# Two column tiles and four sums for the second-half correction of a delta-rule recurrence, and semaphores cleared inside the next block

## Chip, cores and metric

The kernel runs on one core of a Trainium2 chip. The metric is the device time of one execution in microseconds, lower is better. TensorE is PE in the profile (PEld its weight loads), VectorE is DVE, ScalarE is ACT, GpSimd is POOL, and SP is the engine that issues most transfers. A `q` behind an engine's name means its sequencer: waits, branches, drains.

## What is computed

One kernel computes a whole stack for 512 tokens of width 1024: a mixer with a two-directional RWKV-7 recurrence and multi-scale pooling, a product-key expert layer (8 heads, 16 of 16384 experts), a differential-attention layer and a gated-linear-attention layer, each of the two with memory cross-attention and a convolutional feed-forward. The part that the first half of the change touches is the recurrence, cut from the reference:

```python
def wkv7_scan(r, w, k, v, kk, a, reverse):
    def step(state, inp):
        r_t, w_t, k_t, v_t, kk_t, a_t = inp
        sa = jnp.einsum('bhvk,bhk->bhv', state, -kk_t)
        state = (state * w_t[:, :, None, :]
                 + sa[..., :, None] * (kk_t * a_t)[..., None, :]
                 + v_t[..., :, None] * k_t[..., None, :])
        out = jnp.einsum('bhvk,bhk->bhv', state, r_t)
        return state, out
    ...
    _, out = lax.scan(step, state0, xs, reverse=reverse)

for d in range(N_DIR):            # forward, then backward
    ...
    o = o + wkv7_scan(rh, heads(decay), kd, vh, kk, heads(a), reverse=(d == 1))
```

There are 8 heads of 64 channels, two directions, and 512 steps.

## The kernel before

The program is a row of blocks (`nc.Block()`), in each of which every engine runs its own instruction stream and waits on semaphores of the others. A block ends in a barrier of all engines.

**The recurrence** is `mixer_scan`. It works in chunks of 128 steps, four of them (`ST = 4`), and on two heads (`h`) at a time: `m` runs over the four pairs of heads and `d` over the two directions, so there are eight turns, one behind the other. A turn is `solve` and then `steps`. `solve` inverts, for all four chunks and both heads, the triangular matrix of each chunk. It does so by halves of 64 steps: `inverse_t` holds the inverses of the two diagonal 64x64 blocks, made in five levels of products (`E` and `T`, lines L1938 and L1949). Then it applies the inverse to `rhs[d]`, which holds two blocks of 64 columns for each of the two heads, for 128 rows (steps) of each chunk:

- `C{h}` (L1955, copied back by DVE at L1809): the block below the diagonal times the inverse of its half.
- `Y{h}` (L1959): both halves of the right-hand sides times their own inverses. ACT copies the result into `rhs[d]` (L1756).
- `X{h}` (L1965): the correction of the second half, which is the product of `C` with the solved first half, for each chunk. It needs C{h} and Y{h}. DVE adds it to `rhs[d]` (L1813).

`first_half` and `second_half` are rows 0 to 63 and 64 to 127 in the forward direction, and the other way round in the backward one. `ps` are the eight PSUM banks. `steps` then transposes the first columns of `rhs[d]` (`z_t`, L1972), copies the others for the first chunk (`sa0`, L1822), and goes through the four chunks in order, with a state that is handed from one to the next. Between its steps PE, DVE and ACT do pieces of the next turn's front (`beside`): transposes (L1867), and the matrices Lt, L, zk, qb, qk (L1894 to L1900).

Between engines the order is kept by `Steps`: an engine ends each named step with an increment of its semaphore, and the waits count the steps by name. PE's instruction order is the order of the code. An fp32 matmul stands in the trace as two records.

**Semaphores.** Each block takes new ones with `c.semaphore`, which collects them in `c.taken`. When many are in use, `clear_semaphores` (L118 to L122) has POOL clear those in `c.taken` and frees their numbers, behind the barrier that ends a block, and then all engines meet in a second barrier (L121) before the next block begins. `c.apart` holds those that a stream made ahead of time keeps across this. It is called in four places: behind the recurrence, behind the first part of the experts, and behind the attention of each of the two last layers. The blocks that follow are `norm_and_out` (mixer's output, names `gn_`, `out0`), the experts' second part (`ev_`), `residual_split` (`out_`, attention's output product) and `memory_and_out`. Nothing is cleared between the first feed-forward and `project_gla` (names `glav_`).

## Time and profile before

| | us |
|---|---|
| median of 3 runs | 3103.48 |
| lowest and highest | 3098.47, 3103.51 |
| the profiled execution, its own time | 3100.74 |
| its span in the trace | 3099.0 |
| mean granted TensorE clock in it | 0.991 |

The recurrence's eight turns, some 28 us each, lie from 170 to 398 us. The four barriers that `clear_semaphores` adds lie at 398, 1313, 2069 and 2658 us. All times of the trace are from the start of the span. In a timeline row the columns are the start, the time taken together by the rows that it merges, the engine, the line, the operation, what it writes and reads, the count, and in brackets how long the engine sat idle before it and what ended that.

### The profile page before, as it was taken

How to read it: one execution, taken by the hardware profiler on the slowest of the kernel's cores; microseconds unless marked ns; L12 is line 12 of the kernel's file. 1: busy time of each engine (PE TensorE's matmuls, PEld its weight loads, DVE VectorE, ACT ScalarE, POOL GpSimd, SP SyncE). 2: the span in 40 equal slices, each digit the busy share in tenths (PEclk: the TensorE clock that was granted, in tenths of full speed). 3: DMA queues.
4: the chain of work that ended last, by engine and by line, in shares of the span. 5: the costliest groups of instructions: out<-in, count | busy, mean ns of one | idle time of the engine just before them, and what ended most of it. 6: DMA issues, size and time to landing. Idle time of an engine off the chain costs nothing. (4 is left out here: it accounts for less than half of the span.)

```text
span 3099.0 us, 55557 instructions
## 1 busy us (share of the span) xinstructions
PE 3003.1 (97%) x20135; PEld 2648.1 (85%) x20135; DVE 2218.0 (72%) x3931; ACT 965.5 (31%) x1789; POOL 1137.1 (37%) x808
## 2 busy tenths in 40 slices
PE   8999989899999999999999999999999999899999
PEld 6678868799999999999999997768888878588887
DVE  7766687788898898688888886577775345577741
ACT  2444421333434334333333333461211023321110
POOL 5244335222222122144333334214555443245553
PEclk9999999999999999999999999999999999899999
DMA  4100023377878877899999963112223241122333
GB/s 163 34 3 3 3 82 107 118 236 255 297 248 264 287 248 268 289 378 359 349 354 339 352 216 100 38 48 94 96 95 95 79 99 35 55 89 95 99 91 94
DMA packets 241745, 507.91 MB, mean 164 GB/s; under 512 B 44534, under 2 KB 135814, under 8 KB 238124
## 3 DMA queue, kind: packets, MB, share of 16 engines
q1 hardware_dynamic: 182828, 321.11, 31.2%
q0 software_dynamic: 36864, 134.23, 13.3%
q10 hardware_dynamic: 21888, 50.34, 4.2%
q8 instruction: 106, 1.74, 0.2%
q14 instruction: 59, 0.48, 0.0%
HBM read 453.17 MB, written 52.44 MB: 163 GB/s over the span
## 5 line engine op out<-in xcount | busy, mean ns | idle before, releaser
L198 POOL TENSOR_TENSOR up_low<-normed,up_high 128x1024 fp32r<-128x1024 f32 (+1 forms) x136 | 317.2, 2332 | 300.6 <-DVE up_high L193 300.6
L3039 POOL DMA_INDIRECT ev_rows<-in_v,ev_list x128 | 180.1, 1407 | 321.1 <-DVE ev_row_sum L3106 307.7
L203 PE MATMUL up_ps<-ffn_high,up_high 128*128 128x512 f32 x704 | 274.9, 390 | 3.0 <-DVEq L828 3.0
L205 PE MATMUL up_ps<-ffn_high,up_low 128*128 128x512 f32 x704 | 273.9, 389 | 0.0
L204 PE MATMUL up_ps<-ffn_low,up_high 128*128 128x512 f32 x704 | 273.9, 389 | 0.0
L203 PE MATMUL eu_ps<-norm_unit_high,expert_high 128*128 128x384 f32 x768 | 265.4, 346 | 0.0
L205 PE MATMUL eu_ps<-norm_unit_high,expert_low 128*128 128x384 f32 x768 | 257.9, 336 | 0.0
L204 PE MATMUL eu_ps<-norm_unit_low,expert_high 128*128 128x384 f32 x768 | 257.7, 336 | 0.0
L193 DVE CAST up_high<-normed 128x1024 fp32r<-128x1024 f32 (+1 forms) x136 | 91.7, 675 | 206.2 <-PE up_down_ps L205 150.6
L2716 POOL DMA_INDIRECT expert_scores<-in_u,eu_list x64 | 84.2, 1316 | 268.5 <-DVE eu_dots L2744 260.2
L3064 ACT ACTIVATE expert_high<-mixed 128x1024 fp32r<-128x1024 f32 x95 | 100.8, 1061 | 228.9 <-PE ev_acc L205 208.7
L203 PE MATMUL ev_acc<-ev_w_high,expert_high 128*128 128x384 f32 x512 | 171.0, 334 | 0.0
L204 PE MATMUL ev_acc<-ev_w_low,expert_high 128*128 128x384 f32 x512 | 171.0, 334 | 0.0
L205 PE MATMUL ev_acc<-ev_w_high,expert_low 128*128 128x384 f32 x512 | 171.0, 334 | 0.0
L2739 DVE TENSOR_TENSOR expert_low<-eu_turned,expert_high 128x512 fp32r<-128x512 f32 x192 | 123.7, 686 | 64.6 <-ACT expert_high L2833 63.5
L3106 DVE SCALAR_TENSOR_TENSOR ev_row_sum<-ev_rows,ev_weight,ev_row_sum 128x1024 f32<-128x1024 f32 x128 | 164.3, 1285 | 3.9 <-DMA ev_rows<-in_v,ev_list 3.9
L2843 ACT ACTIVATE mixed<-eu_ps 128x384 f32<-128x384 f32 x128 | 62.9, 491 | 328.1 <-PE eu_ps L205 328.1
L2716 POOL DMA_INDIRECT normed<-in_u,eu_list x64 | 68.8, 1075 | 255.5 <-DVE eu_dots L2744 254.9
L786 ACT ACTIVATE mixed<-up_ps,columns_sb 128x512 f32<-128x512 f32 x88 | 68.6, 780 | 297.2 <-DVE up_ps L816 297.2
L3099 DVE TENSOR_TENSOR expert_low<-mixed,expert_high 128x1024 fp32r<-128x1024 f32 x95 | 118.4, 1246 | 58.6 <-ACT expert_high L3064 58.6
L203 PEld LDWEIGHTS up_ps<-ffn_high,up_high 128*128 128x128 f32 x704 | 132.2, 188 | 31.5 <-DVEq L828 3.7
L204 PEld LDWEIGHTS up_ps<-ffn_low,up_high 128*128 128x128 f32 x704 | 132.2, 188 | 27.8 <-issue 0.5
(709 smaller groups left out, 8615.5 us busy)
## 6 DMA issues: line engine op xcount, KB each, us to landing
mixed<-in_v SPq DMA_DIRECT2D x128, 512.0 KB
normed<-in_u SPq DMA_DIRECT2D x125, 512.0 KB
normed<-in_w_up SPq DMA_DIRECT2D x88, 512.0 KB, 3.4
expert_act<-mixed ACTq DMA_DIRECT2D x128, 192.0 KB
expert_gates<-eu_gates ACTq DMA_DIRECT2D x24, 1024.0 KB
expert_scores<-expert_gates SPq DMA_DIRECT2D x16, 1536.0 KB
normed<-expert_act SPq DMA_DIRECT2D x128, 192.0 KB
normed<-in_w_down SPq DMA_DIRECT2D x32, 448.0 KB, 3.3
```

The lines of the kernel that those rows point to most:

```text
L193: return nc.vector.tensor_copy(high.bitcast(F32R), of)
L198: return nc.gpsimd.tensor_tensor(low.bitcast(F32R), of, high, ALU.subtract)
L203: nc.tensor.matmul(out, w_high.bitcast(F32R), x_high.bitcast(F32R), start=start, stop=False)
L204: nc.tensor.matmul(out, w_high.bitcast(F32R), x_low.bitcast(F32R), start=False, stop=False)
L205: return nc.tensor.matmul(out, w_low.bitcast(F32R), x_high.bitcast(F32R), start=False, stop=stop)
L786: nc.scalar.activation(cv[:, s, :], ps[s][:, :], ACT.Identity, scale=c.cols[:, bass.ds(j + at + 2 * 2 * FT, 1)], bias=c.cols[:, bass.ds(j ...
L2716: nc.gpsimd.indirect_dma_start(rows[b % 4], None, u, bass.IndirectOffsetOnAxis(ap=list_[:, b % 8:b % 8 + 1], axis=0)).then_inc(fetched[b % ...
L2739: nc.vector.tensor_tensor(low[b % SLOTS][:, ks, :].bitcast(F32R), ps_u[n][:, :, :], high[b % SLOTS][:, ks, :], ALU.subtract).then_inc(low_ ...
L3039: nc.gpsimd.indirect_dma_start(rows[:, b % 4, :], None, v, bass.IndirectOffsetOnAxis(ap=list_[:, b % 8:b % 8 + 1], axis=0)).then_inc(fetch ...
L3064: nc.scalar.activation(high[b % SLOTS][:, :, :].bitcast(F32R), raw[:, b % 4, :, :], ACT.Copy).then_inc(high_made, 1)
L3099: nc.vector.tensor_tensor(low[b % SLOTS][:, :, :].bitcast(F32R), raw[:, b % 4, :, :], high[b % SLOTS][:, :, :], ALU.subtract).then_inc(low ...
L3106: nc.vector.scalar_tensor_tensor(out=row_sum[:, b % 2, :], in0=rows[:, b % 4, :], scalar=weight[:, bass.ds(i * per + b, 1)], in1=row_sum[: ...
```

## The change

In the recurrence, the correction of the second half changes on PE and DVE. Before, PE makes the four chunks of head 0 as soon as C0 and Y0 are there, all into the same 64 output rows, and then those of head 1. Afterwards PE waits for C and Y of both heads and then goes through the chunks in two groups of two (`p`). In each chunk it makes head 0 and head 1 one behind the other, each in output rows (and so columns of the array) of its own: `column_tile[d][0]` is the second half, `column_tile[d][1]` the first. There are still eight matmuls. The two groups have banks of their own (`x_bank`). DVE makes four sums (X0 to X3), each of two chunks of one head, where it made two of four chunks. Head 1's sums read PSUM rows of the other half than those that they write. The steps behind wait for X3 in place of X1.

The second part: `clear_semaphores` becomes `retire_semaphores`, which only renames the list, and `clear_stale`, which POOL runs as its first action in the next block. The second barrier is gone in all four places. There is a fifth retirement, behind the first feed-forward, whose clearing lies in `project_gla`; so that this one is possible, the semaphores of the stream and of the norm that live on are set apart in `build`.

```diff
-def clear_semaphores(nc, c):
-    nc.clear_and_free_semaphores(c.taken)
-    nc.all_engine_barrier()
-    c.taken, c.apart = c.apart, []
+def retire_semaphores(c):
+    assert not c.stale
+    c.stale, c.taken, c.apart = c.taken, c.apart, []
+
+def clear_stale(nc, c):
+    nc.clear_and_free_semaphores(c.stale)
+    c.stale = []
...
             @block.gpsimd
             def _(pool):
+                clear_stale(nc, c)
...
+        x_bank = ((ps[3], ps[1]), (ps[4], ps[5]))
+        column_tile = ((half[1], half[0]), (half[0], half[1]))
...
-                    for h in range(2):
-                        mine = rhs[d][second_half[d], :, h:4:2, :]
-                        pe_s[d].wait(dve, m, f"X{h}")
-                        done.ends(nc.vector.tensor_tensor(mine, pair(c_bank[h][second_half[d], :, :]), mine, ALU.add), f"X{h}")
+                    for p in range(2):
+                        for h in range(2):
+                            mine = rhs[d][second_half[d], 2 * p:2 * p + 2, h:4:2, :]
+                            pe_s[d].wait(dve, m, f"X{2 * p + h}")
+                            done.ends(nc.vector.tensor_tensor(mine, pair(x_bank[p][h][column_tile[d][h], 0:2, :]), mine, ALU.add), f"X{2 * p + h}")
...
                     for h in range(2):
                         dve_s[d].wait(pe, m, f"C{h}")
                         act_s[d].wait(pe, m, f"Y{h}")
-                        for t in range(ST):
-                            ins = nc.tensor.matmul(c_bank[h][two_, t, :], square[one, ST * h + t, HEAD:P], rhs[d][one, t, h:4:2, :], start=True, stop=True)
-                        pe_s[d].ends(ins, f"X{h}")
+                    for p in range(2):
+                        for t in (2 * p, 2 * p + 1):
+                            for h in range(2):
+                                ins = nc.tensor.matmul(x_bank[p][h][column_tile[d][h], t % 2, :], square[one, ST * h + t, HEAD:P], rhs[d][one, t, h:4:2, :], start=True, stop=True)
+                                if t % 2:
+                                    pe_s[d].ends(ins, f"X{2 * p + h}")
```

PE, first turn, from the last products Y to the transposes for z_t. `L1965` is X before, `L1978` after; `L1867` the next turn's first transposes; `L1972` and `L1986` z_t. Before:

```order
628 L1959 MATMUL scan_ps<-scan_rhs,scan_inverse_t 64x128 x8
629 L1965 MATMUL scan_ps<-scan_rhs,normed 64x128 [waits scan_scalar_done0,scan_vector_done0]
630 L1965 MATMUL scan_ps<-scan_rhs,normed 64x128 x3
631 L1965 MATMUL scan_ps<-scan_rhs,normed 64x128 [waits scan_scalar_done0,scan_vector_done0]
632 L1965 MATMUL scan_ps<-scan_rhs,normed 64x128 x3
633 L1867 MATMUL scan_ps<-ident,scan_ez 128x128 [waits scan_vector_done1]
634 L1867 MATMUL scan_ps<-ident,scan_ez 128x128 x3
635 L1972 MATMUL scan_ps<-ident,scan_rhs 128x128 [waits scan_vector_done0]
```

After:

```order
628 L1970 MATMUL scan_ps<-scan_rhs,scan_inverse_t 64x128 x8
629 L1978 MATMUL scan_ps<-scan_rhs,normed 64x128 [waits scan_vector_done0,scan_scalar_done0]
630 L1978 MATMUL scan_ps<-scan_rhs,normed 64x128 x7
631 L1878 MATMUL scan_ps<-ident,scan_ez 128x128 [waits scan_vector_done1]
632 L1878 MATMUL scan_ps<-ident,scan_ez 128x128 x3
633 L1986 MATMUL scan_ps<-ident,scan_rhs 128x128 [waits scan_vector_done0]
```

All waits for C and Y, of both heads, now stand ahead of the first of the eight products.

POOL, around the end of the recurrence and the first product of `norm_and_out` (L120 before and L127 after is the clearing). Before:

```order
134 L1704 UNCONDITIONAL_BRANCH
135 L120 ISA [waits barrier_Pool_Activation_PE_DVE_SP_gather]
136 L1469 UNCONDITIONAL_BRANCH [waits barrier_Pool_Activation_PE_DVE_SP_gather]
137 L198 TENSOR_TENSOR out_low<-normed,out_high 128x512 [waits in_x_loaded0] x12
```

After, at this place, and then at the start of `project_gla`, where nothing was cleared before:

```order
134 L1714 UNCONDITIONAL_BRANCH
135 L1476 UNCONDITIONAL_BRANCH [waits barrier_Pool_Activation_PE_DVE_SP_gather]
136 L127 ISA
137 L204 TENSOR_TENSOR out_low<-normed,out_high 128x512 [waits out0_high_made] x12
...
307 L738 UNCONDITIONAL_BRANCH
308 L4617 UNCONDITIONAL_BRANCH [waits barrier_Pool_Activation_PE_DVE_SP_gather]
309 L127 ISA x3
310 L204 TENSOR_TENSOR glav_low<-normed,glav_high 128x128 [waits ev_w_low_made]
```

One of the two meetings of all engines is gone, and the clearing stands behind the other, in POOL's own stream. In `project_gla` three clearings come ahead of POOL's first work.

## Rows read from the trace of the kernel before

**Rows 1.** The page: busy time, share of the span and instructions of each engine.
```profile
PE 3003.1 (97%) x20135; PEld 2648.1 (85%) x20135; DVE 2218.0 (72%) x3931; ACT 965.5 (31%) x1789; POOL 1137.1 (37%) x808
```

**Rows 2.** Stretches: length; busy PE, PEld, DVE, ACT, POOL; clock; DMA share, GB/s.
```profile
399.00:402.40 3.40, 3.25 (x4) 1.51 (x5) 3.18 (x7) 2.57 (x5) 0.30 (x1) 0.50 0.66 219
1313.80:1317.10 3.30, 3.21 (x10) 3.21 (x11) 2.30 (x4) 2.62 (x4) 1.99 (x3) 0.50 0.60 171
...
173.80:398.80 225.00, 215.78 (x5064) 194.86 (x5056) 143.06 (x399) 89.19 (x286) 81.66 (x79) 1.00 0.01 3
```

**Rows 3.** Timeline, second turn, from ACT's copy of Y0 to z_t.
```profile
219.78 0.60 ACT L1756 ACTIVATE scan_rhs<-scan_ps 128x512 f32<-128x512 f32 x1 [1.96 <-PE scan_ps L1959]
...
220.52 1.93 PE L1965 MATMUL scan_ps<-scan_rhs,normed 64*64 64x128 f32 x16
220.65 0.60 ACT L1756 ACTIVATE scan_rhs<-scan_ps 128x512 f32<-128x512 f32 x1 [0.28 <-PE scan_ps L1959]
221.61 0.68 DVE L1813 TENSOR_TENSOR scan_rhs<-scan_ps,scan_rhs 64x512 f32<-64x512 f32 x1 [1.31 <-PE scan_ps L1965]
...
222.48 0.68 DVE L1813 TENSOR_TENSOR scan_rhs<-scan_ps,scan_rhs 64x512 f32<-64x512 f32 x1 [0.19 <-PE scan_ps L1965]
...
223.22 0.66 PE L1972 MATMUL scan_ps<-ident,scan_rhs 128*128 128x128 f32 x4 [0.19 <-DVE scan_rhs L1813]
```

**Rows 4.** Line L1965 alone: count, shortest, median and longest in ns, first and last start.
```profile
L1965 PE MATMUL scan_ps<-scan_rhs,normed x128: 269/269/292, 192.9 to 388.4; 64*64 64x128 f32 x128
```

**Rows 5.** Timeline, PE, matmuls that lie on several tiles of the array.
```profile
198.29 0.69 PE L1894 MATMUL scan_ps<-scan_ez,scan_bb 64*64 64x64 f32 x32
...
199.20 0.39 PE L1992 MATMUL scan_ps<-normed,scan_v_n 128*64 128x128 f32 x4
```

**Rows 6.** Line L1790 alone: DVE operations that read 256 PSUM columns.
```profile
L1790 DVE TENSOR_TENSOR normed<-scan_ps,scan_block_lower x16: 414/420/426, 175.3 to 366.3; 128x256 f32<-128x256 f32 x16
```

**Rows 7.** Timeline, DVE: two of these back to back.
```profile
199.06 0.76 DVE L1790 TENSOR_TENSOR normed<-scan_ps,scan_block_lower 128x256 f32<-128x256 f32 x2 [0.29 <-PE scan_ps L1894]
```

**Rows 8.** ACT's sequencer at the first and last clearing: end-of-block release, then second barrier's.
```profile
L1704 ACTq EVENT_SEMAPHORE x1: 17/17/17, 397.8 to 397.8; - x1
...
L121 ACTq EVENT_SEMAPHORE x1: 17/17/17, 398.7 to 398.7; - x1
...
L4079 ACTq EVENT_SEMAPHORE x1: 17/17/17, 2657.3 to 2657.3; - x1
...
L121 ACTq EVENT_SEMAPHORE x1: 17/17/17, 2658.8 to 2658.8; - x1
```

**Rows 9.** POOL's three clearings at the last place.
```profile
L120 POOLq DRAIN  x3: 93/113/115, 2657.4 to 2658.2; - x3
L120 POOLq EVENT_SEMAPHORE_RANGE_CLEAR  x3: 200/243/261, 2657.5 to 2658.3; - x3
```

**Rows 10.** Timeline: what starts the work behind the first clearing, in `norm_and_out`.
```profile
399.15 2.08 PE L1482 MATMUL gn_dev<-mix_o,gn_centre 128*128 128x512 f32 x2 [2.16 <-DVE gn_centre L1602]
...
402.83 0.60 ACT L1538 ACTIVATE gn_sq<-gn_dev 128x512 f32<-128x512 f32 x1 [0.91 <-PE gn_dev L1483]
```

**Rows 11.** Timeline: PE's first work behind the second clearing, and DVE's next operand.
```profile
1313.89 0.69 PE L203 MATMUL ev_acc<-expert_first_w_high,expert_high 128*128 128x384 f32 x1 [3.01 <-DVEq L3120]
...
1316.12 0.55 DVE L3101 TENSOR_TENSOR ev_w_low<-ev_weighed,ev_w_high 128x384 fp32r<-128x384 f32 x1
...
1316.94 0.45 PE L203 MATMUL ev_acc<-expert_first_w_high,expert_high 128*128 128x384 f32 x1
```

**Rows 12.** Timeline: POOL's first work behind the last clearing, and at `project_gla`; PE there.
```profile
2658.95 1.53 POOL L3452 TENSOR_TENSOR mixed<-mixed,at_r 128x512 f32<-128x512 f32 x1 [34.47 <-POOLq L121]
...
2479.93 3.31 POOL L198 TENSOR_TENSOR glav_low<-normed,glav_high 128x128 fp32r<-128x128 f32 x3 [7.95 <-DVE glav_high L193]
2480.45 0.41 PE L203 MATMUL glav_ps<-ffn_high,glav_high 128*16 128x512 f32 x1 [1.98 <-POOL glav_low L198]
```

**Rows 13.** Timeline, PE: the longest idle stretch that no half-clock stretch followed within 5 us.
```profile
1884.25 0.50 PE L203 MATMUL qkv_ps<-qkv_x_high,qkv_high 128*128 128x512 f32 x1 [1.91 <-POOL qkv_low L198]
```

25 lines of the change are left out of this document (16 added, 9 removed).

## The prediction

> **What bounds the kernel now.** I read the page first: PE is busy for 97% of the span [rows 1], so over most of the 3099 us only less PE work, or PE starting sooner behind a stop, moves the end. Then I read the stretch that the first half of the change touches. From 173.8 to 398.8 us PE is busy for 215.8 of 225.0 us at full clock [rows 2], but that is mostly the length of short matmuls that wait their turn: in the timeline of one turn [rows 3] PE, DVE and ACT hand one another each step, DVE idles 1.31 us ahead of the first sum, PE waits for the second. All eight turns read alike to 0.02 us at this place. POOL is ahead: it is busy for 82 of the 225 us. So what happens between the products Y and the transposes z_t lies on the path of each of eight turns. Last I read what lies around the four clearings: no engine but POOL has anything to do there.
>
> **First half: the correction X.** Count from ACT's copy of Y0, which starts at 219.78 and takes 0.60 [rows 3]. Before: PE starts X at 220.52, that is 0.14 behind the copy's end. Its 16 records (8 matmuls) take 1.93 us, one alone 0.27 [rows 4], so they start (1.93 - 0.27) / 15 = 0.11 apart. DVE's first sum starts at 221.61, while PE is still at head 1; the second, at 222.48, waits for the last product and takes 0.68; z_t starts at 223.22. From the start of X to z_t: 2.70 us.
>
> Afterwards the start moves. X now waits for the copy of Y1, which starts at 220.65, and ends at 221.25; plus 0.14, X starts at 221.39, which is *0.87 later* than 220.52. What hid this wait before was PE's own work on Y1 and on head 0's products; now nothing does.
>
> What PE gains: do two matmuls that read the same rows but fill different columns of the array run side by side? [rows 5] show this in this kernel: the four records of L1992 take 0.39 us, where one behind the other they would need 0.27 + 3 x 0.11 = 0.60, and the 32 of L1894, 64 columns each on four quarters of the array, take 0.69. I take full pairing. The first group of two chunks is four records per tile, so X0 and X1 end 3 x 0.11 + 0.27 = 0.60 behind the start, a first record's 0.02 added 0.62; the last of all at 7 x 0.11 + 0.29 = 1.06, where it took 1.93.
>
> What DVE does with it: 0.04 behind X0 the sums begin, at 0.66. A sum now has 256 columns in place of 512. The nearest row for 256 PSUM columns is 0.42 us [rows 6], against 0.68 for 512 [rows 3]; two of them back to back take 0.76 together, so that a second one starts 0.34 behind the first [rows 7]. Four sums: 3 x 0.34 + 0.42 = 1.44 us, where the two long ones needed 1.36. X2 and X3 are there by 1.10, when DVE is at its second sum, so DVE is the one that ends last: 0.66 + 1.44 = 2.10, and z_t at 0.05 behind that, 2.15. Against 2.70 this gives back 0.55 us.
>
> Sum per turn: 0.87 - 0.55 = **+0.3 us**, and times 8 turns **+2.5 us**, slower. The bounds: if a sum's wait keeps it from starting until the one ahead is over, four sums cost 4 x 0.42 + 3 x 0.02 = 1.74, and a turn +0.6 (together +5). If the tiles don't pair, X0 ends only at 1.2 and X3's products at 2.0, z_t comes at 2.6 or so, +0.75 a turn (+6). On the other side, if DVE's sums pair better than in [rows 7], PE's end of 1.06 + 0.04 and one last sum of 0.42 is the floor, z_t at 1.55 and -0.3 a turn (-2.3). No row shows a DVE operation whose two operands lie in different halves of the partitions, as head 1's sums have; I put it at nothing, since no row prices it; the upper bound covers 0.15 us for each of the 16.
>
> The Trainium skill has a rule that speaks against this half: TensorEngine Tiling (Array Packing), section PSUM Bottleneck, says that tiling speeds up TensorE but not the evacuation of PSUM, and that the copy may become the bound. The trace agrees as far as it can: the sums cost 1.36 of the 2.70 us already. By that rule the gain of the pairing is capped by the sums, as in the sum above; without it one would count PE's 0.87 us a turn as gain.
>
> **Second half: the clearings.** At the first one ACT is released from the block's end at 397.8 and from the second barrier at 398.7; at the last one at 2657.3 and 2658.8 [rows 8]. These are 0.9 and 1.5 us; the two between them read alike as 1.3 and 1.2. Sum: 4.9 us in which nobody works. All of it goes for PE, DVE, ACT and SP. POOL still clears, about 0.11 + 0.24 us for each range and some idle time between [rows 9], so POOL gains only the second meeting, some 0.3 us at the last place. Place by place:
> - 398 us, *-0.9 or more*. POOL's first work comes four microseconds later. There is more to it: PE's idle stretch of 2.16 us [rows 10] shrinks to 1.3. Behind the 2.16 the granted clock fell to 0.50, that is 1.2 GHz, from 399 to 402.4 [rows 2]. No idle stretch of up to 1.91 us [rows 13] but one of 1.89 was followed by such a fall. If it stays away, PE's first four matmuls, which ACT waits for (0.91 us idle [rows 10]), take half of the 3.4 us. DVE is what that block runs on, and it waits for ACT's square of them. ACT can't start it before its weight copy, about 0.9 earlier than now, so I take -1.8.
> - 1313 us, *-1.3*. The expert block behind it is PE's, without a gap until 1845, so all of it counts. PE's idle 3.01 us [rows 11] become 1.7, and here too the clock may stay at 2.4 GHz, but DVE has its next operand only from 1316.12 to 1316.67 (L3101), and PE takes it at 1316.94 [rows 11]: at most 0.4 more. I take -1.5.
> - 2069 us, *-1.2*: PE waits for a DVE operation there (idle 4.68 us), POOL is close behind. I take -1.2.
> - 2658 us, *-0.3 to -1.5*: POOL's first product at 2658.95 [rows 12] comes no more than 0.35 earlier, and ACT, DVE and PE wait for it, but PE's own first matmuls, at half clock, come 1.45 earlier. I take -1.
> - 2479 us, *+0.6*: `project_gla` clears anew. POOL starts its first product at 2479.93, 0.5 behind the release, and PE waits for it (idle 1.98 [rows 12]). Three clearings cost about 1.2 us [rows 9], of which 0.5 lie in POOL's wait for DVE; POOL is then late by 0.6.
>
> Sum: -1.8 - 1.5 - 1.2 - 1.0 + 0.6 = **-4.9 us**, bounds -2.5 and -7.5.
>
> **Total.** +2.5 - 4.9 = -2.4 us. Against the profiled execution's own 3100.7 (its span 3099.0 and 1.7 around it) that gives 3098.3; the median of the three runs is 2.7 above it, so I forecast 3103.5 - 2.4 = **3101 us**. A measurement of this kernel tells 0.2%, that is 6.2 us, from no change; three runs alone spread over 5 us.
>
> **The rivals.**
> 1. *The correction gains as meant.* DVE's four short sums overlap with PE and with one another to the floor above, -0.3 a turn, -2.3 us; with -4.9 of the clearings, and the fall of the clock gone at both places, -7 to -10: 3095. For it: PE's stretch is halved. Against it: the start moves by 0.87, which is in the code, and DVE's 1.36 of sums don't shrink. Chance 0.15.
> 2. *Slower: the clock in the recurrence.* In each turn PE now stands idle for 0.8 us ahead of X and for about as long between X and z_t (1.1 us, part of it filled by the next turn's transposes), with 1.1 us of work between. In the whole stretch from 173.8 the clock was 1.00 [rows 2]. If this thinner pattern brings a fall to half of the 3.4 us length that is seen at 399, matmuls that start 0.11 apart then start 0.21 apart; PE has about a third of such a stretch on the path, so about 1.2 us a turn. It decides from the point where it happens in six or more of eight turns: 8 x 1.2 + 2.5 - 4.9 = +7: 3111. Against it: idle stretches of the same length stand in `steps` and in other blocks with no fall behind them. Chance 0.06.
> 3. *The tiles don't pair, or the sums don't overlap*: +5 to +6 in place of +2.5; total 0 to +1: 3104. Chance 0.14.
> 4. *The barriers' time is taken back.* What starts sooner waits for a transfer or for POOL all the same; only half of the 4.9 us arrives: total +0.1: 3103.5. Chance 0.12. The engines' streams, transfers too, all start sooner, which speaks against it.
>
> My own forecast has 0.53. **Range**: 3094 to 3108, which takes in rivals 1, 3 and 4 and the run-to-run spread. Chances: faster by over 0.2% 0.17 (rival 1 and the tail of the forecast), same 0.76, slower by over 0.2% 0.07 (rival 2 and a little).
>
> **What would show it.** In the timeline of a turn: X starts 0.14 behind the second copy of Y, not the first; its 16 records take about 1.1 us; four sums of about 0.42, 0.34 apart; from the start of the first copy of Y to z_t 3.7 us where it is 3.44. A turn lasts 0.3 us longer; the recurrence ends 2.4 us later. No second barrier; PE's idle stretch of 1.3 us at the first place and 1.7 at the second, and a granted clock of 1.00 behind both. PE's wait at `project_gla` 2.6 us. I am wrong if the turn is shorter than before, if the granted clock within the recurrence falls below 1, or if the stages behind the clearings last as much longer as the barriers were.

## The result

The changed kernel takes 3107.7 us (median of 20 runs, 3101.8 to 3114.2), the kernel before, beside it on the same chip, 3102.7 us (20 runs, 3098.5 to 3106.8). The ratio is 1.0016 with an interval of 1.0009 to 1.0022: it is **slower, by 0.16%, 5.0 us**, where the prediction had it faster by 2.4 us. The time lies just inside the range (3094 to 3108). The difference is below the 0.2% that was called the limit of the measurement, but over 20 runs each its interval lies wholly above 1: it is a loss, not a gain.

The profiled execution of the changed kernel takes 3110.0 us. Its page, first part, answers to [rows 1]:

```profile
PE 3007.8 (97%) x20135; PEld 2648.6 (85%) x20135; DVE 2218.6 (71%) x3947; ACT 966.2 (31%) x1789; POOL 1133.0 (36%) x808
```

The engines do the same work, but for DVE's 16 additional sums; PE is "busy" 4.7 us longer with the same 20135 matmuls, a first hint at a lower clock. The second turn, from the second copy of Y to z_t, is the counterpart of [rows 3] (timeline: start, time, engine, line, operation, what it writes and reads, count, idle time before):

```profile
221.18 0.60 ACT L1766 ACTIVATE scan_rhs<-scan_ps 128x512 f32<-128x512 f32 x1 [0.28 <-PE scan_ps L1970]
...
221.92 1.09 PE L1978 MATMUL scan_ps<-scan_rhs,normed 64*64 64x128 f32 x16 [0.79 <-ACT scan_rhs L1766]
222.58 1.78 DVE L1824 TENSOR_TENSOR scan_rhs<-scan_ps,scan_rhs 64x256 f32<-64x256 f32 x4 [1.75 <-PE scan_ps L1978]
222.94 0.66 PE L1878 MATMUL scan_ps<-ident,scan_ez 128*128 128x128 f32 x4
...
224.41 0.69 PE L1986 MATMUL scan_ps<-ident,scan_rhs 128*128 128x128 f32 x2 [0.81 <-DVE scan_rhs L1824]
```

X takes 1.09 us in place of 1.93 and starts 0.14 behind the second copy's end, both as forecast. The four sums take 1.78 us together, not 1.44. PE now stands idle for 0.79 us ahead of X and for 0.81 ahead of z_t. From the start of the first copy to z_t it is 4.11 us in each turn, where it was 3.45. And in the stretches (length; busy PE, PEld, DVE, ACT, POOL; clock; DMA share, GB/s), the counterpart of [rows 2]:

```profile
169.68:398.80 229.12, 211.62 (x5010) 191.09 (x5010) 141.58 (x400) 90.22 (x284) 81.65 (x79) 0.97 0.01 3
398.80:410.50 11.70, 10.67 (x78) 7.83 (x78) 4.05 (x15) 1.11 (x4) 0.00 (x0) 0.50 0.01 1
224.10:227.50 3.40, 3.09 (x24) 2.72 (x24) 1.67 (x6) 0.73 (x2) 0.00 (x0) 0.50 0.00 0
254.80:258.20 3.40, 3.40 (x27) 2.74 (x26) 1.40 (x4) 0.60 (x1) 0.00 (x0) 0.50 0.00 0
1325.20:1338.00 12.80, 12.75 (x73) 12.75 (x74) 10.20 (x14) 5.80 (x9) 7.60 (x7) 1.00 0.97 339
```

The granted clock, 1.00 from 173.8 us to the end of the recurrence before [rows 2], is 0.50 (1.2 GHz) for 3.4 us in three of the eight turns (at 224.1, 254.8 and 312.8) and again from 398.2 to 415.3, over the end of the recurrence and into the next block. At the experts' second part it is the other way round: at 1.00 where it was 0.50.

Stage by stage, from the release of one block to that of the next (us; "clearings alone" is an experiment below):

| stage | before | after | difference | clearings alone | forecast |
|---|---|---|---|---|---|
| recurrence | 227.9 | 240.8 | +12.9 | 229.0 | +2.5 |
| `norm_and_out`, its barrier included | 65.8 | 65.4 | -0.4 | 63.3 | -1.8 |
| experts' second part, its barrier included | 538.5 | 535.0 | -3.5 | 535.0 | -1.5 |
| block at 2068 | 50.1 | 49.5 | -0.6 | 49.4 | -1.2 |
| block at 2657 | 78.0 | 76.8 | -1.3 | 76.9 | -1.0 |
| `project_gla` | 95.6 | 96.3 | +0.7 | 95.9 | +0.6 |

The rows add up to +7.8; what the change doesn't touch differs by +1.5 between the two profiled executions, which makes the 9.3 us between their spans. The table sets one execution beside one: the changed one took 2.3 us more than the median of its kernel, the one before 1.9 less, so the differences here are larger than the 5.0 us between the medians. The stages behind the recurrence gave 5.1 us (7.6 with the clearings alone), where 4.9 was expected. The loss is in the recurrence, five times as large as forecast, and it has two parts. One is in every turn: 8 x 0.65 = 5.2 us, forecast 2.5. The other goes with the clock, 7.7 us: the three turns with a half-clock stretch are some 1.5 us longer each than the same turns without (4.5), and from the last z_t to the block's end it is 11.6 us in place of 8.35 (3.2).

The fall over the end is not the change's alone. Besides the one before, five of the kernels below have the recurrence exactly as before. In two of these six executions the clock fell over the end too, for 6.8 us, and the recurrence lasted 230.3 us in place of 227.9. In pe_kept_busy:

```profile
391.70:398.50 6.80, 6.72 (x52) 5.01 (x53) 2.40 (x9) 0.56 (x2) 0.00 (x0) 0.50 0.01 2
```

None of the six had a fall within the turns.

### The profile page after: what moved, and what is told of

Its sections match the earlier page's. It is cut to its first block and busy times, and to the rows that moved or that the text cites. A ratio compares the mean times of both kernels' runs of the same rounds, so it can differ in the third digit from the quotient of the medians.

```text
span 3108.3 us, 55530 instructions
## 1 busy us (share of the span) xinstructions
PE 3007.8 (97%) x20135; PEld 2648.6 (85%) x20135; DVE 2218.6 (71%) x3947; ACT 966.2 (31%) x1789; POOL 1133.0 (36%) x808
## 3 DMA queue, kind: packets, MB, share of 16 engines
q1 hardware_dynamic: 182828, 321.11, 30.7%
## 5 line engine op out<-in xcount | busy, mean ns | idle before, releaser
L2730 POOL DMA_INDIRECT normed<-in_u,eu_list x64 | 68.8, 1076 | 255.4 <-DVE eu_dots L2758 254.8
L211 PEld LDWEIGHTS up_ps<-ffn_high,up_low 128*128 128x128 f32 x704 | 132.1, 188 | 27.8
```

Of the source, the lines that this page charges most:

```text
L211: return nc.tensor.matmul(out, w_low.bitcast(F32R), x_high.bitcast(F32R), start=False, stop=stop)
L2730: nc.gpsimd.indirect_dma_start(rows[b % 4], None, u, bass.IndirectOffsetOnAxis(ap=list_[:, b % 8:b % 8 + 1], axis=0)).then_inc(fetched[b % ...
```

## The experiments

Sixteen kernels ran, all but the first four to answer a question that the runs ahead of them had left. Ratios are to the kernel before on the same chip.

### The two halves apart

**x_only**: the correction X as changed, the clearings as before. **clear_only**: the clearings as changed, X as before. 

> The kernel before with the correction of the recurrence as in the change (wait for both heads, two column tiles, four sums) and the second barriers left in. Theory A (the correction costs by itself): from the first copy of Y to z_t 4.11 us in place of 3.45 in all eight turns, and the granted clock falls to half in some of the turns, where such a turn is some 1.4 us longer still; the recurrence ends 5 to 13 us later, and with the barriers left in the time is +7 to +12 us, ratio 1.002 to 1.004. Theory B (the falls of the clock come from the clearings or from where the free time lies, not from the correction): turns of 28.25 and 28.7 us only, clock 1.00 from 174 to 398 us, time +5 us. Theory C (the loss lies behind the clearings): within 1 us of the kernel before.

Measured: 3114.9 us against 3102.3, ratio 1.0034 [1.0022, 1.0046]. Recurrence 242.0 us, four turns with a half-clock stretch, and half clock from 402.1 over its end.

> The kernel before with the clearings moved into the next blocks and the second barriers gone, the correction as before. Theory A: the turns are as before (27.6 and 28.0 us), the recurrence ends at the same time, and behind it 4 to 6 us are gained, ratio 0.998 to 0.9987; the clock behind the expert block's start stays at 1.00. Theory C (the freed time is given back by the blocks behind): ratio 1.000, and the stages behind the four places longer by what the barriers took.

Measured: 3095.6 us, ratio 0.9975 [0.9964, 0.9985]. The recurrence has its turns as before and full clock from 175.4 us on; it lasts 229.0 us because its first 6 us, ahead of all that the change touches, ran at half clock. The other stages of the table shorten by 7.6 us together. So the changed kernel is a gain of 7 to 8 us and a loss of 10 to 13 in one (6.7 and 12.6 by the medians, 0.25% and 0.34% by the ratios); alone, each is clear of the noise.

### What in X costs time: the wait or the sums

**wait_both**: the kernel before, its X head by head on one half of the columns, but both heads' copies are waited for first.

```diff
                     for h in range(2):
                         dve_s[d].wait(pe, m, f"C{h}")
                         act_s[d].wait(pe, m, f"Y{h}")
+                    for h in range(2):
                         for t in range(ST):
                             ins = nc.tensor.matmul(c_bank[h][two_, t, :], square[one, ST * h + t, HEAD:P], rhs[d][one, t, h:4:2, :], start=True, stop=True)
```

> The kernel before with one edit: PE waits for C and Y of both heads ahead of the first product X; one tile and two long sums as before. Theory A: X starts 0.87 us later and all behind it as well, 4.32 us from the first copy of Y to z_t, eight turns +7 us; and if it is PE's idle time ahead of X that lets the clock fall, half-clock stretches of 3.4 us show in the recurrence here too, each +1.4 us. If the idle time between X and z_t is what counts, it is no longer than before here, and the clock stays at 1.00: +7 us alone, ratio 1.0023.

Measured: 3110.5 us, ratio 1.0022 [1.0013, 1.0031]. The row of PE, second turn:

```profile
222.63 1.93 PE L1966 MATMUL scan_ps<-scan_rhs,normed 64*64 64x128 f32 x16 [0.79 <-ACT scan_rhs L1756]
```

z_t comes 4.32 us behind the start of the first copy, +0.87 a turn: the price that the prediction put on the later start is right to 0.01 us, and with two long sums and X untiled all of it arrives. The recurrence lasts 237.6 us, with the turns as expected. The same 0.79 us idle stands ahead of X here as in the changed kernel, but with 1.93 us of products behind it the clock held from 174.5 to 396.4; only behind that, over the end, was it at half.

**four_sums**: the kernel before, X head by head as before, only its two sums cut into four of two chunks, each with its own wait.

```diff
                     for h in range(2):
-                        mine = rhs[d][second_half[d], :, h:4:2, :]
-                        pe_s[d].wait(dve, m, f"X{h}")
...
+                        for p in range(2):
+                            mine = rhs[d][second_half[d], 2 * p:2 * p + 2, h:4:2, :]
+                            pe_s[d].wait(dve, m, f"X{2 * h + p}")
```

> The kernel before with four sums of two chunks each, but head by head on one tile: PE starts head 0 as soon as C0 and Y0 are there, as before, and signals after each two chunks. Theory A (what counts is that PE starts early and DVE follows it closely): sums start 0.62 behind the start of X and then 0.44 to 0.45 apart, at PE's pace; z_t 2.44 to 2.50 us behind the start of X in place of 2.70, a turn 0.2 to 0.26 us shorter, clock 1.00 throughout the recurrence, in all -1.6 to -2.1 us, ratio 0.9994. Rival (each sum's fixed cost is what counts, four cost more than two): +0.1 us a turn or more, +1 us.

Measured: 3099.8 us, ratio 0.9991 [0.9982, 1.0000]. z_t comes 3.18 us behind the start of the first copy, where it was 3.45; the recurrence lasts 225.9 us, -2.0, with full clock from 173.1 on. By the trace short sums alone are a gain (the ratio's interval reaches 1.0000): the last one has half as much to do when PE is done. One thing more stands in this trace. The barrier behind the recurrence is in place, and yet the clock didn't fall there (length; busy PE, PEld, DVE, ACT, POOL; clock; DMA share, GB/s), and `norm_and_out` lasted 64.1 us, where it was 65.8:

```profile
396.00:461.00 65.00, 57.05 (x222) 41.02 (x223) 58.84 (x80) 21.98 (x36) 27.25 (x18) 1.00 0.30 99
```

### Is it PE's idle time that lets the clock fall?

**filled**: the changed kernel, with six matmuls of 64 x 64, whose result nobody reads, on PE ahead of its wait for X, and six more between X and its wait ahead of z_t. **fill_ahead** has only the first six, **fill_behind** only the second.

```diff
+                    for _ in range(6):
+                        nc.tensor.matmul(ps[6][half[0], 0, 0:HEAD], inverse_t[half[0], 0, :], inverse_t[half[0], 1, :], start=True, stop=True)
                     for h in range(2):
                         dve_s[d].wait(pe, m, f"C{h}")
                         act_s[d].wait(pe, m, f"Y{h}")
...
+                    for _ in range(6):
+                        nc.tensor.matmul(ps[6][half[0], 0, 0:HEAD], inverse_t[half[0], 0, :], inverse_t[half[0], 1, :], start=True, stop=True)
```

> The changed kernel, with six small matmuls (64 x 64, their result is read by nobody) on PE ahead of its wait for the correction X, and six more between X and its wait ahead of z_t. They take nothing away, they only keep PE busy in the two idle stretches of about 0.8 us that each turn has. Theory A (the clock falls because the tiled X leaves PE thinly busy): the granted clock stays at 1.00 from 174 to the end of the recurrence and behind it, the periods are 28.2 to 28.7 in all turns where they are 28.25 to 30.1 now, and the recurrence lasts 231 to 233 us in place of 240.8, so the kernel comes out near 3099, a ratio of 0.999. Rival B (the fall has to do with the column tiles themselves, or with what comes behind the turn's end): the stretches at half clock stay where they are and the recurrence lasts 240 us or more; each turn is longer by what the small matmuls hold up PE, if at all. Rival C (even with the clock full the start of X and the four sums cost +0.65 us a turn): both hold, then 8 x 0.65 = 5.2 us remain of the recurrence's 12.9.

Measured: 3101.1 us, ratio 0.9997 [0.9987, 1.0006]; by the ratios that is 6 us better than the changed kernel (1.0016, and the intervals don't touch) with nothing but more work on PE. The timeline of the second turn and the stretches:

```profile
220.98 0.60 ACT L1766 ACTIVATE scan_rhs<-scan_ps 128x512 f32<-128x512 f32 x1 [0.27 <-PE scan_ps L1970]
221.73 1.09 PE L1980 MATMUL scan_ps<-scan_rhs,normed 64*64 64x128 f32 x16
222.38 1.78 DVE L1824 TENSOR_TENSOR scan_rhs<-scan_ps,scan_rhs 64x256 f32<-64x256 f32 x4 [1.75 <-PE scan_ps L1980]
...
223.33 0.91 PE L1987 MATMUL scan_ps<-scan_inverse_t 64*64 64x64 f32 x12
...
224.22 0.66 PE L1990 MATMUL scan_ps<-ident,scan_rhs 128*128 128x128 f32 x4
```
```profile
173.00:394.80 221.80, 215.84 (x5191) 196.74 (x5190) 141.77 (x401) 88.53 (x281) 81.66 (x79) 1.00 0.01 3
394.80:404.10 9.30, 8.39 (x75) 6.22 (x74) 3.79 (x13) 1.11 (x4) 0.00 (x0) 0.63 0.00 0
```

PE no longer idles at either place, z_t comes 4.11 us behind the first copy as before (the matmuls hold nothing up), and the clock is 1.00 from 173.0 to 394.8; from z_t to z_t it is 28.25 and 28.70 us by turns, as in those turns of the changed kernel that had no fall, and 27.4 to the last one. The recurrence lasts 234.8 us in place of 240.8. One thing of the expectation missed: the clock still fell for 6.8 us at the very end, behind 394.8, where the last turn has nothing of a next turn beside it and PE idles for 1.1 us behind the small matmuls. It lasted 234.8 us, not the 231 to 233 expected; 227.9 + 5.2 would have been 233.1 without that fall.

> As the one before, but only the six small matmuls ahead of X; between X and z_t PE stands idle as in the changed kernel. If the idle stretch ahead of X is the one that counts (the wait for the second head's copy put it there): no stretch at half clock in the recurrence, which lasts 231 to 233 us. If the other does: three or more stretches of 3.4 us at half clock as in the changed kernel, and 240 us. If it takes both, something between.

Measured: recurrence 234.6 us, one half-clock stretch in it (225.9 to 229.3) and none over its end; 3101.5 us in one run.

> As two before, but only the six small matmuls between X and the wait ahead of z_t. If the idle stretch ahead of z_t is the one that counts: no stretch at half clock in the recurrence, which lasts 231 to 233 us. If the one ahead of X does: stretches at half clock stay, and the recurrence lasts about 240 us.

Measured: recurrence 234.6 us, one half-clock stretch in it (309.8 to 313.3) and none over its end; 3097.3 us in one run. The two stretches:

```profile
225.90:229.30 3.40, 3.40 (x27) 2.74 (x26) 1.40 (x4) 0.60 (x1) 0.00 (x0) 0.51 0.02 5
309.80:313.20 3.40, 3.40 (x26) 2.72 (x24) 1.65 (x6) 0.60 (x1) 0.00 (x0) 0.51 0.00 0
```

So neither idle stretch is *the* one: filling either left one fall where there were three, filling both left none within the turns. That PE's idle time brings the falls is shown by the two intervals of `filled` and of the changed kernel; how the falls divide between the places is not, with one execution of each.

The other kernels of this document say the same, one execution each. Add up PE's idle time from its last product Y to z_t in a turn (the last turn left out), and count the falls within the turns. At 0.2 us or less (nine kernels, `filled` among them): none. At 0.8 to 1.0: none in wait_both and sums_64, one in fill_ahead and fill_behind. At 1.2: one in sums_128 and one in sums_128_waits. At 1.6: three in the changed kernel, four in x_only, two in two_waits.

### Why the four sums stay 0.45 us apart

The prediction had them 0.34 apart by [rows 7]. Four kernels take the possible reasons one by one. In **sums_64** the four sums of the kernel `four_sums` stand behind one wait, for the last product. **sums_128** does the same over all 128 partitions: each product is made for both halves of the columns, 16 matmuls in place of 8, and one of the halves is multiplied by zero as it is added. **sums_128_waits** puts a wait ahead of each of these. **two_waits** is the changed kernel with waits only ahead of its first and third sum.

```diff
+                    pe_s[d].wait(dve, m, "X3")
                     for h in range(2):
                         for p in range(2):
                             mine = rhs[d][second_half[d], 2 * p:2 * p + 2, h:4:2, :]
-                            pe_s[d].wait(dve, m, f"X{2 * h + p}")
```
```diff
                     for p in range(2):
+                        pe_s[d].wait(dve, m, f"X{2 * p + 1}")
                         for h in range(2):
                             mine = rhs[d][second_half[d], 2 * p:2 * p + 2, h:4:2, :]
-                            pe_s[d].wait(dve, m, f"X{2 * p + h}")
```

> The kernel before in all but the correction X: each product is made for both halves of the columns (16 matmuls in place of 8, the second half's result is multiplied by a column that is zero there and so changes nothing), and the four sums of two chunks each go over 128 partitions in place of 64, one multiply-add each, all behind the last product. The question is the distance between the starts of DVE's sums. Theory A (sums that span all 128 partitions are taken up before the one ahead is over, those of 64 partitions are not): they start 0.34 to 0.36 apart at about 0.42 each, the 0.08 that the row of L1790 shows. Rival B (the distance has to do with the sums' wait for PE, or with reading PSUM): they are 0.44 apart as in the kernel with four sums over 64 partitions. The kernel as a whole is slower than before, by the products that are made twice: PE needs some 2.9 us for X, the sums all start behind it, z_t comes 1 to 2 us later a turn; this run is for the distance alone.

> The kernel before with its correction's two sums cut into four of half the chunks over 64 partitions, all four behind one wait, for the last product; between them stands no wait. The distance of the starts is the question: 0.43 to 0.45 apart with a duration of 0.42 if sums over 64 partitions are never taken up before the one ahead is over (Theory A); 0.34 if it was the wait ahead of each sum that kept them apart (Rival B). A turn's sums start only behind the last product, so z_t comes 0.5 us later than with a wait for each, near 3.7 us behind the start of the first copy of Y.

> The changed kernel, but DVE waits for PE only ahead of the first and of the third sum (for the products of both heads) and not ahead of the second and the fourth. Theory A (the wait that stands ahead of each sum keeps it from starting until the one ahead is over): sums start 0.34 apart within a pair and 0.42 to 0.45 from pair to pair, z_t comes 3.9 us behind the start of the first copy of Y in place of 4.11, and a period without half clock is 28.05 in place of 28.25. Rival B (it is the operands, which lie in different halves of the partitions for head 1): still 0.45 apart, 4.11. The granted clock in the recurrence falls in some turns as in the changed kernel, since PE's idle stretches are nearly as long.

> The kernel with sums over 128 partitions behind one wait (0.39 apart at 0.476 each), now with a wait ahead of each sum, all of them met by then. Theory A (a wait alone keeps a sum from starting early, whatever its partitions): 0.49 to 0.51 apart. Rival B (it takes the wait and 64 partitions together, as the solve's steps of 128 partitions overlap by 0.055 with a wait ahead of each): 0.42 apart.

The rows of DVE, for four sums together, of sums_128, sums_64 and two_waits in this order:

```profile
223.80 1.66 DVE L1817 SCALAR_TENSOR_TENSOR scan_rhs<-scan_ps,upper_eq,scan_rhs 128x256 f32<-128x256 f32 x4 [2.22 <-PE scan_ps L1971]
```
```profile
223.32 1.41 DVE L1816 TENSOR_TENSOR scan_rhs<-scan_ps,scan_rhs 64x256 f32<-64x256 f32 x4 [2.19 <-PE scan_ps L1969]
```
```profile
223.34 1.78 DVE L1824 TENSOR_TENSOR scan_rhs<-scan_ps,scan_rhs 64x256 f32<-64x256 f32 x4 [1.79 <-PE scan_ps L1978]
```

One of these sums lasts 0.476, 0.42 and 0.42 us. So their starts lie (1.66 - 0.476) / 3 = 0.39, (1.41 - 0.42) / 3 = 0.33 and (1.78 - 0.42) / 3 = 0.45 apart: in the first two kernels each starts 0.08 us before the one ahead is over, in the third 0.03 behind it. sums_128_waits reads 0.39 as well, with waits (0.49 to 0.51 or 0.42 were expected, neither came). This throws out three reasons in turn. It isn't the 64 partitions: sums_64 overlaps (my theory there fell). It isn't the wait: two_waits does not overlap within its pairs, which have none (my theory fell again), and sums_128_waits overlaps with one ahead of each. It isn't PSUM, which all of them read. What is left, and what only the changed kernel and two_waits have, is the column tiles: head 0's product lies in the same half of the partitions as its sum and head 1's in the other, and the sums take them by turns. (The order of the sums differs as well, but the step from the second to the third goes to the other two chunks and the other head in sums_64 too, and there it is 0.33, here 0.45 to 0.46.) A row that was in the trace of before all along fits it: the pair of L1841, whose first operation works on partitions 0 to 63 and whose second on 64 to 127, last 0.28 and 0.29 us, and together

```profile
339.31 0.58 DVE L1841 SCALAR_TENSOR_TENSOR scan_state<-scan_ps,scan_f,scan_decayed 64x64 f32<-64x64 f32 x2
```

that is, with no overlap at all. Neither of these two crosses the halves within itself, so in this pair the change of half from one operation to the next is enough. No run shows a crossing without a change: whether it adds anything in the changed kernel, where both come together, stays open.

A side result: one wait for all costs more than it saves. In sums_64 the sums are 0.1 us closer together, but start 1.3 us later than in `four_sums`, and z_t comes at 4.2 us (3.7 was expected). A second one: sums_128 makes twice the products X, for both halves of the columns, and X takes 1.96 us in place of 1.93, not the 2.9 expected: products on different columns run side by side. The four kernels as a whole, one run each beside one of the kernel before: 3115.0 us against 3105.4 (sums_128), 3111.2 against 3104.0 (sums_64), 3109.1 (two_waits) and 3112.0 (sums_128_waits) against 3102.8; they were made for the distances alone.

### Where the experts' second part gets its 3.5 us

The barrier is 1.3 of it. The rest looked like the clock: from PE's first product to its 25th it is 5.8 us with the half-clock stretch behind 1313.8 [rows 2] and 4.3 without. **pe_kept_busy** and **pe_busier** are the kernel before with matmuls nobody reads while POOL clears; the second has more of them, and some at the end of the block before.

```diff
+        with nc.psum_tensor("idle_ps", [P, P], F32) as idle:
+            for _ in range(4):
+                nc.tensor.matmul(idle[:, :], c.ident[:, :], c.ident[:, :], start=True, stop=True)
         clear_semaphores(nc, c)
```

> The kernel before, clearings and barriers as they are, with four matmuls of 128 x 128 (result read by nobody) on PE while POOL clears the semaphores ahead of the experts' second part (1312.3 to 1313.5). PE's idle stretch of 3.01 us there becomes one of some 1.4 and one of some 0.6. Theory A (of the 3.6 us that the clearings' change gained in this stage, 1.3 are the barrier's and 2.2 come from the granted clock, which no longer falls at 1313.8): no stretch at half clock behind 1313.8, and the stage from block to block lasts 538.5 - 2.2 = 536.3 us with the barrier in place. Rival B (the 3.6 us come from the earlier start of PE or of the transfers, not from the clock): the clock stays up but the stage lasts 538 us or more. Rival C: the clock falls all the same, then its cause isn't PE's idle stretch.

Measured: the clock fell all the same, 0.4 us behind PE's first product, though no idle stretch ahead of it was longer than some 1.4 us; the stage lasted 538.5 us (the kernel 3106.4 in one run).

```profile
1316.70:1320.10 3.40, 3.40 (x13) 3.40 (x12) 2.73 (x4) 2.21 (x4) 2.35 (x3) 0.50 0.81 230
```

> The kernel before with matmuls nobody reads on PE at the block change ahead of the experts' second part: four at the end of the part before (1310.9 to 1311.9) and six while POOL clears (1312.3 to 1313.5), so that of PE's idle 3.01 us about 1 is left, in three pieces. With four of them in the middle alone the granted clock still fell, 0.4 us later. Theory A (this stage's extra gain of 2.3 us, beyond the barrier's 1.3, is the fall of the clock that stays away): no half clock here, the stage from block to block is 536.3 us in place of 538.5 with the barrier in place. Rival B (the gain comes from PE's and the transfers' earlier start): clock at 1.00, the stage still 538 or more. If the clock falls again, the question stays open.

Measured: the clock stayed at 1.00, the first 24 products took 4.3 us, and the stage was no shorter (the kernel took 3103.1 us in one run): from PE's first product to its last 536.1 us, where before has 535.9 and after 533.7. PE gave the 1.5 us back, waiting:

```profile
1327.55 0.41 PE L203 MATMUL ev_acc<-ev_w_high,ev_high 128*128 128x384 f32 x1 [0.62 <-DVE ev_w_low L3104]
...
1333.26 0.41 PE L203 MATMUL ev_acc<-expert_first_w_high,expert_high 128*128 128x384 f32 x1 [1.28 <-DVE expert_first_w_low L3104]
```

Before has one such wait, after has none. Behind DVE stand the transfers: ACT takes up the fourth tile of rows of v when it has landed. The rows of ACT, before and after:

```profile
1325.93 1.06 ACT L3064 ACTIVATE expert_high<-mixed 128x1024 fp32r<-128x1024 f32 x1 [3.88 <-DMA mixed<-in_v]
```
```profile
1335.39 1.06 ACT L3079 ACTIVATE expert_high<-mixed 128x1024 fp32r<-128x1024 f32 x1 [1.97 <-DMA mixed<-in_v]
```

That is 12.0 us behind PE's first product before (1313.89) and 10.1 us after (1325.25). What could let the same load land earlier? POOL's gathers use the same transfer engines: from 1313 to 1334 us before, the queue that holds SP's loads took 61.4% of the 16 engines' time and that of the gathers 30.7%. The clearing inside the block delays the gathers: POOL issues the first one 0.84 us behind PE's first product before and 1.77 after:

```profile
1314.73 0.97 POOL L3039 DMA_INDIRECT ev_rows<-in_v,ev_list  x1 [0.92 <-POOL ev_list L3032]
```
```profile
1327.02 1.39 POOL L3054 DMA_INDIRECT ev_rows<-in_v,ev_list  x1 [0.92 <-POOL ev_list L3047]
```

**late_gathers** is the kernel before with a memset of 0.95 us on POOL ahead of its first gather, **busier_late** is pe_busier with the same.

```diff
+                nc.gpsimd.memset(rows[:, 0, :], 0.0).then_inc(held, 1)
+                pool.wait_ge(held, 1)
                 take_list(0, 0)
                 fetch(0, 0)
```

> The kernel before with a memset of 128 x 1024 on POOL (0.95 us) ahead of its first list at the start of the experts' second part, so that POOL's gathers are issued 1.8 us behind PE's first product in place of 0.8, as they are with the clearing inside the block. Theory A (the gathers and SP's loads of the rows of v share the transfers, and early gathers hold up SP's loads, for which PE waits at 12 and 18 us): ACT takes up the fourth tile of v at about 10 us behind PE's first product in place of 12.0, PE has no wait over 0.45 us in the first 20 us, and as the clock still falls the stage gains those 0.8 us: 537.7 from block to block. Rival B (the gathers have nothing to do with it): the fourth tile at 12 to 14 us, PE's wait of 0.6 to 1.6 us at 18 us stays, 538.5.

> The kernel whose PE is kept busy at this block change (no fall of the clock), with the same memset on POOL ahead of its first gather; the barrier and the clearing stay ahead of the block. There the clock at 1.00 saved 1.5 us in the first 24 products, and PE lost 2.6 us again in two waits for rows of v at 12 and 17.5 us. Theory A (the loads of v set the pace of the first 20 us, and late gathers let them come sooner): no such waits, the part from PE's first product to its last lasts 533.7 us as with the clearings inside the block, in place of 536.1. Rival B: the waits stay, 535 to 537 us.

Measured, in us, one execution each (the first row is the kernel before and seven others that have this stage as before):

| kernels | clock behind the first product | gather | fourth tile at | first to last product |
|---|---|---|---|---|
| before and seven like it | half | 0.8 | 11.7 to 15.2 | 535.5 to 537.5 |
| pe_busier | full | 0.8 | 13.9 | 536.1 |
| late_gathers | half | 1.8 | 11.7 | 535.7 |
| busier_late | full | 1.8 | 10.6 | 534.5 |
| after and six like it | full | 1.8 | 9.8 to 12.1 | 533.7 to 535.0 |

Neither of the two brings more than 0.3 us alone, both together 1.4 of the 2.2 us. The likeliest reading is that in the first 20 us of this stage PE and the loads of v limit it in turn: a faster clock is only worth something when the loads come sooner, and they only matter when PE is fast enough to meet them. It is argued, not shown. Kernels with equal code here differ by up to 3.5 us in the tile's arrival and by up to 2.0 us in the stage, and the tile came at 11.7 with the late gathers of late_gathers and in the earliest kernel with early ones alike. The expectations fit in part: in late_gathers PE's wait at 18 us was gone, as theory A had it, but the fourth tile was not at 10 us and the stage lasted 538.3 us, not 537.7; for busier_late both were off (533.7, or 535 and more). The kernels took 3104.1 and 3100.2 us, one run each, against 3099.7. The last 0.8 us stay open.

### The better kernel

**four_sums_clear**: the clearings as changed, and X head by head with its four sums, the two parts that were found to gain.

> The changed kernel with its clearings inside the blocks, but the correction X as in the kernel before (head by head, one half of the columns, X starts behind the first copy of Y), and only its two sums cut into four of half the chunks. If the two halves of the change add up, this is the best of both: the recurrence lasts 225.9 us (as with the four sums alone, against 227.9 before), no stretch at half clock within it, and the stages behind the clearings are shorter by the 7.6 us seen with the clearings alone, together about 9.6 us: 3093, a ratio of 0.997. Rival: the block behind the recurrence gets back the fall of the granted clock as it ends at another moment, then the sum is 7 to 8 us and the ratio 0.9975.

Measured: 3093.7 us (6 runs) against 3103.4 (16 runs), ratio **0.9967 [0.9955, 0.9979]**, 9.7 us faster than before and, by the two ratios, 15 us faster than the change as made. The second turn:

```profile
220.40 1.93 PE L1977 MATMUL scan_ps<-scan_rhs,normed 64*64 64x128 f32 x16
220.53 0.60 ACT L1766 ACTIVATE scan_rhs<-scan_ps 128x512 f32<-128x512 f32 x1 [0.28 <-PE scan_ps L1970]
221.06 1.73 DVE L1824 TENSOR_TENSOR scan_rhs<-scan_ps,scan_rhs 64x256 f32<-64x256 f32 x4 [0.88 <-PE scan_ps L1977]
...
222.84 0.66 PE L1984 MATMUL scan_ps<-ident,scan_rhs 128*128 128x128 f32 x4
```
```profile
174.50:395.60 221.10, 214.58 (x5036) 194.23 (x5028) 145.47 (x414) 89.04 (x284) 81.65 (x79) 1.00 0.01 3
395.80:458.90 63.10, 55.83 (x216) 39.88 (x216) 57.49 (x77) 20.58 (x34) 27.25 (x18) 1.00 0.30 100
```

X is long, 1.93 us, and that costs nothing: it starts 0.87 us earlier, the sums run beside it, and PE has no idle stretch in it. The clock is at 1.00 from 174.5 us to the end of the recurrence (225.6 us) and in the block behind.

## Why the prediction was wrong

Two terms of its sum failed: the clock in the recurrence, which the sum put at nothing and which cost 7.7 us in the traced execution, and DVE's four sums, put at 1.44 us and measured at 1.78. The first turned a gain into a loss.

**The start of X, +0.87: right.** wait_both measures it alone.

**PE's pairing: right.** 1.09 us measured, 1.06 forecast.

**Four sums in 1.44 us: wrong, the step that made the turn +0.65 in place of +0.3.** They take 1.78. With X0 at 0.66 behind X's start, as forecast, that is the whole difference: 0.66 + 1.78 + 0.05 = 2.49 from X to z_t, forecast 2.15. The step took its distance of 0.34 from two operations that work on the same partitions [rows 7] and applied it to four that change sides. The prediction had noted that no row shows a sum across the halves, and set it at nothing; the pair of L1841 in the same trace shows two neighbours on different halves without overlap, and was not read. The upper bound of this term, +0.6 a turn, had it right. The rule that the prediction weighed, from the Trainium skill (TensorEngine Tiling (Array Packing), section PSUM Bottleneck), that tiling doesn't speed up what empties PSUM, fits these traces: of the 0.84 us that PE gained in a turn none arrived. From the start of X to z_t it is 2.49 us with X tiled and four sums, and 2.44 in four_sums, with X untiled; what the turn won against the 2.70 of before comes from the shorter sums.

**The clock in the recurrence: named as rival 2, at 0.06, and the larger part of the loss.** The sum had no term for it. Its mechanism, idle ahead of X and ahead of z_t, is what `filled` shows; whether the little work between them counts by itself was not tried. Its sizes were off on both sides: a fallen turn costs 1.5 us, not 1.2; it happened in three turns of eight, not in six or more; and a place was missed, the end of the recurrence, where the fall lasted longest and cost 3.2 us, though a shorter one, worth 2.2 us, came there in two of six executions of the unchanged recurrence as well. The argument against it was that idle stretches of the same length stand elsewhere with no fall behind them, and, with [rows 13], that a stretch of 1.91 us had none. That looked at one stretch at a time. In the changed kernel no stretch here is longer than 0.82 us, but for 1.4 in the last turn; wait_both has the same 0.79 ahead of X, and but 0.2 ahead of z_t, and keeps its clock in all turns up to the end; pe_kept_busy lost it behind stretches of 1.4 and 0.5 us. In these runs the falls go with how much PE stands idle in a neighbourhood, not with its longest stretch.

**The clearings: right in sign and too small, -7.6 alone where -4.9 was forecast (-7.5 the bound).** At 398 the forecast of -1.8 became -2.5 where the recurrence kept its clock, and -0.4 in the changed kernel, because its own fall reached into that block. Of the 2.5 some 1.7 are the fall of the clock and 0.9 the barrier: four_sums, with the barrier and without the fall, has 64.1 us, between 65.8 and the 63.2 of four_sums_clear; the forecast had put 0.9 on the fall. At 1313 the step "DVE has its next operand only from 1316.12, at most 0.4 more" was wrong: PE's first 24 products ran without a pause in 4.3 us in the changed kernel, 1.5 us sooner than before; -3.5 in place of -1.5. What kept the gain, most likely the loads of v, is not settled. The places at 2068 (-0.6 for -1.2), 2657 (-1.3 for -1.0) and 2479 (+0.7 for +0.6) make up little.

**The sum.** Forecast +2.5 - 4.9 = -2.4. With the turn's +0.65 and the clearings at their measured -7.6, and without any fall of the clock, it would have been 5.2 - 7.6 = -2.4 as well: two errors that cancel. The clock alone turned the sign. The medians say it too, as an estimate: the 5.0 us of the changed kernel are 7.4 more than -2.4, the 12.6 of x_only are 7.4 more than 5.2, and `filled`, without falls in the turns, comes out at -2.3 (by the ratios x_only is 5.3 more than 5.2, and `filled` at -0.9). That the time still fell inside the range is luck. The range ended at 3108 because rival 2 was priced at 3111 and then left out with its 0.06.

## What to carry to other kernels

When a change makes PE's work shorter in a loop in which the engines wait for one another, add up how much PE stands idle in the whole neighbourhood, not the longest stretch: work that lies beside DVE's anyway was free here and kept the clock, so there was nothing to win by packing it. Before two products are put on different tiles, look where their results come to lie, and what their consumers then have to do. And try the halves of a change apart: here one was worth about -7 us and the other about +12, and what gained in the second was its least conspicuous part, the short sums.

## What the runs showed of the hardware

- DVE started a sum about 0.08 us before the one ahead was over where both worked on the same partitions, be it 64 (sums_64) or 128 (sums_128, and sums_128_waits with a met wait ahead of each). Where the operands changed between the halves of the partitions it did not: 0.03 us of pause in the changed kernel and in two_waits.
- The granted clock fell to 0.50 in a loop whose idle stretches are 0.8 us each, and twelve small matmuls a turn that nobody reads, put into them, kept it at 1.00 within the turns and took 6 us off the recurrence.
- Sixteen products X (64x128 each), spread over both halves of the columns, took 1.96 us in sums_128; eight on one half took 1.93 in four_sums.
- The fall doesn't come at every turn, nor at the same turns in each kernel: three of eight in the changed kernel, four in x_only, one when either stretch is filled. The end of the recurrence had one in two of six executions with that code unchanged.
- With the gathers at 0.8 us and PE at full clock the fourth tile of the loads was taken up at 13.9 us, with the gathers at 1.8 us at 10.6; at half clock it was 12.0 and 11.7. One execution each: that the gathers hold up the loads is not shown.
